# Sample attention: probabilities instead of values as the streamed operand, and the turning step dropped

## The reference

```python
def sparse_attend(q, k_sel, v_sel, dist, rel_bias):
    ...
    p = jax.nn.softmax(s, axis=-1)
    o = jnp.einsum('bthgn,btnhd->bthgd', p.astype(v_sel.dtype), v_sel)
    return o.reshape(B, T, A_WIDTH)
...
def mem_kv(mem, g_mem, w_xk, w_xv):
    m = rms_norm(mem, g_mem)
    mk = jnp.einsum('bmd,de->bme', m, w_xk).reshape(B, M, X_HEADS, X_HEAD_DIM)
    mv = jnp.einsum('bmd,de->bme', m, w_xv).reshape(B, M, X_HEADS, X_HEAD_DIM)
```

## Time and profile before

| | before |
|---|---|
| median of 3 runs | 2934.78 us |
| time of the profiled execution | 2934.78 us |
| its span | 2933.2 us |
| TensorE busy | 2777.6 us (95%) |
| VectorE busy | 1666.7 us (57%) |
| ScalarE busy | 1068.3 us (36%) |
| GpSimd busy | 212.6 us (7%) |
| mean granted TensorE clock | 0.974 |

### The profile page before, as it was taken

How to read it: one execution, slowest core, us unless ns; L and a number is a source line. 1 busy time by engine, 2 the same in 40 slices (tenths; PEclk the granted TensorE clock), 3 DMA queues, 4 the chain that set the end, 5 groups by cost and what they waited for, 6 DMA issues and landing times.

```text
span 2933.2 us, 46674 instructions
## 1 busy us (share of the span) xinstructions
PE 2777.6 (95%) x18724; PEld 2626.1 (90%) x18724; DVE 1666.7 (57%) x2355; ACT 1068.3 (36%) x1331; POOL 212.6 (7%) x303
## 2 busy tenths in 40 slices
PE   8989999899999999999989977989999999899995
PEld 7879887799999999998979856979999999899994
DVE  4464564477878777787454423365555555543334
ACT  4233454344444443444342323333232232333332
POOL 0102211011111111110000000000000000000002
PEclk9999999999999999999999988989999999999998
DMA  9756646745555454554545565535555555445553
GB/s 284 146 145 178 203 160 206 230 135 154 144 138 151 130 158 130 159 145 124 144 143 144 205 236 176 150 121 151 150 146 154 143 153 147 125 118 147 149 153 100
DMA packets 692709, 460.24 MB, mean 157 GB/s; under 512 B 13455, under 2 KB 661231, under 8 KB 686319
## 3 DMA queue, kind: packets, MB, share of 16 engines
q1 hardware_dynamic: 679952, 414.25, 49.4%
q0 software_dynamic: 8960, 30.47, 3.9%
q10 hardware_dynamic: 3712, 14.35, 1.3%
HBM read 429.91 MB, written 29.13 MB: 156 GB/s over the span
## 4 chain that ended last, share of the span: by engine, by line
PE 91%; DVE 3%; DMA 3%; ACT 2%; issue 1%; POOL 1%; POOLq 0%; ACTq 0%; SPq 0%; DVEq 0%
PE psum L580 19%; PE psum L586 19%; PE psum L577 19%; PE psum L816 4%; PE psum L1170 4%; PE psum L1171 3%; PE psum L1172 3%; PE psum L981 2%; PE psum L821 2%; PE psum L959 1%; PE psum L1072 1%; DMA ring<-in_w_in 1%; PE psum L962 1%; PE psum L955 1%; DMA h<-in_cache_mem_v 1%
## 5 line engine op out<-in xcount | busy, mean ns | idle before, releaser
L1211 DVE TENSOR_TENSOR w_low<-ring,w_high 128x2048 fp32r<-128x2048 f32 x292 | 675.5, 2314 | 387.3 <-ACT w_high L1841 386.9
L1841 ACT ACTIVATE w_high<-ring 128x2048 fp32r<-128x2048 f32 x294 | 561.6, 1911 | 776.1 <-PE psum L586 589.3
L577 PE MATMUL psum<-x_high,w_high 128*128 128x320 f32 x3808 | 609.5, 312 | 2.9 <-ACT w_high L1841 2.9
L580 PE MATMUL psum<-x_high,w_low 128*128 128x320 f32 x3808 | 601.5, 310 | 8.5 <-DVE w_low L1211 8.5
L580 PEld LDWEIGHTS psum<-x_high,w_low 128*128 128x128 f32 x3808 | 571.8, 189 | 9.1 <-DVE w_low L1211 9.0
L577 PEld LDWEIGHTS psum<-x_high,w_high 128*128 128x128 f32 x3808 | 568.9, 188 | 10.6 <-issue 3.5
L586 PE MATMUL psum<-h_low,w_high 128*128 128x320 f32 x3360 | 527.7, 309 | 0.0
L586 PEld LDWEIGHTS psum<-h_low,w_high 128*128 128x128 f32 x3360 | 502.4, 188 | 0.0
L1170 PE MATMUL psum<-y_high,w_down_high 128*128 128x320 f32 x704 | 219.7, 312 | 15.9 <-DVE w_low L1773 15.9
L1171 PE MATMUL psum<-y_low,w_down_high 128*128 128x320 f32 x704 | 217.9, 310 | 0.0
L1172 PE MATMUL psum<-y_high,w_low 128*128 128x320 f32 x704 | 217.9, 310 | 0.0
(11 more groups left out here) (394 smaller groups left out, 3033.6 us busy)
## 6 DMA issues: line engine op xcount, KB each, us to landing
ring<-in_w_in SPq DMA_DIRECT2D x128, 1024.0 KB, 5.6
ring<-in_w_up SPq DMA_DIRECT2D x88, 1024.0 KB, 5.6
ring<-in_w_down SPq DMA_DIRECT2D x64, 704.0 KB, 4.7
ring<-in_w_xk SPq DMA_DIRECT2D x16, 1024.0 KB, 5.3
ring<-in_w_xv SPq DMA_DIRECT2D x16, 1024.0 KB, 5.1
ring<-in_w_out SPq DMA_DIRECT2D x16, 1024.0 KB, 5.9
ring<-in_w_xq SPq DMA_DIRECT2D x16, 1024.0 KB, 5.8
ring<-in_w_xo SPq DMA_DIRECT2D x16, 1024.0 KB, 5.9
```

Of the source, the lines that this page charges most:

```text
L577: mm(out, w_hi[:, j % 2, k, :], x_hi[:, k, :], start=k == 0, stop=False)
L580: mm(out, w_lo[:, j, k, :], x_hi[:, k, :], start=False, stop=False)
L1211: V.tensor_tensor(w_lo[:, j], ring[:, j], w_hi[:, j % 2].bitcast(FP32), ALU.subtract).then_inc(N.slab_lo, 1)
L1841: F(w_hi[:, j % 2], ring[:, j], ACT.Copy).then_inc(N.slab_hi, 1)
```

## The change

The operands of `sample_weigh` are exchanged: the page of values (128 by 128) becomes the stationary operand, and the strip of 32 columns of `probT` is streamed. The result has columns of tokens at once, on all 128 partitions, each KV head in 32 columns of the bank. The number of matmul calls stays 12 for a sequence. The loop over heads is now the outer one. `sample_turn` and `sample_rows` go, with the semaphore `o_rows` and the buffer; `sample_weighed(b-1)` reads bank 6 and stands where `sample_rows(b-1)` stood. In the setup, the third step of `small_in` gets a semaphore of its own, `diag_ready`, and the later counts of `small_in` fall by one.

```diff
             def sample_weigh(b):
                 pe.wait_ge(N.p_evac, H + b + 1)
-                pe.wait_ge(N.o_evac, H)
-                pe.wait_ge(N.o_rows, b)
+                pe.wait_ge(N.o_evac, H + b)
                 pe.wait_ge(v_loaded[b % 2], 32 * (b // 2 + 1))
-                for pg in range(NPG):
-                    for h in range(KVH):
-                        mm(bank(6)[32 * h:32 * h + 32, 0:P], probT[:, b % 2, pg * P + 32 * h:pg * P + 32 * h + 32],
-                           v_page[:, b % 2, pg, h * P:(h + 1) * P], start=pg == 0, stop=False, skip_group_check=True)
                 for h in range(KVH):
-                    last = mm(bank(6)[32 * h:32 * h + 32, 0:P], probT[0:NS, b % 2, 2 * P + 32 * h:2 * P + 32 * h + 32],
-                              vN[0:NS, 2, h * P:(h + 1) * P], start=False, stop=True, skip_group_check=True)
+                    oc = slice(32 * h, 32 * h + 32)
+                    for pg in range(NPG):
+                        mm(bank(6)[:, oc], v_page[:, b % 2, pg, h * P:(h + 1) * P],
+                           probT[:, b % 2, pg * P + 32 * h:pg * P + 32 * h + 32], start=pg == 0, stop=False)
+                    last = mm(bank(6)[:, oc], vN[0:NS, 2, h * P:(h + 1) * P],
+                              probT[0:NS, b % 2, 2 * P + 32 * h:2 * P + 32 * h + 32], start=False, stop=True)
                 last.then_inc(N.pv_mm, 1)
-
-            def sample_turn(b):
-                pe.wait_ge(N.o_rows, b + 1)
-                pe.wait_ge(N.o_evac, H + b)
-                tr(bank(7)[:, 0:P], o_rows, ident).then_inc(N.pv_mm, 1)
...
-                if b > 1:
-                    sample_turn(b - 2)
                 memory_slab(R + H + b)
...
-            sample_turn(DB - 2)
             memory_slab(28)
             sample_weigh(DB - 1)
-            memory_slab(29)
-            sample_turn(DB - 1)
-            for n in range(30, 32):
+            for n in range(29, 32):
                 memory_slab(n)
...
             def sample_prob_out(b):
                 act.wait_ge(N.p_T, H + b + 1)
-                if b >= 2:
-                    act.wait_ge(N.pv_mm, ROWS_AT[b - 2])
-                else:
-                    act.wait_ge(N.pv_mm, H + b - 1)
+                act.wait_ge(N.pv_mm, H + b - 1)
...
-            def sample_rows(b):
-                act.wait_ge(N.pv_mm, ROWS_AT[b])
-                if b:
-                    act.wait_ge(N.pv_mm, TURN_AT[b - 1])
-                F(o_rows, bank(6)[:, 0:P], ACT.Copy).then_inc(N.o_rows, 1)
-
             def sample_weighed(b):
-                act.wait_ge(N.pv_mm, TURN_AT[b])
-                F(zq[:, :, SEQ + b * DT:SEQ + (b + 1) * DT], bank(7)[:, 0:P].rearrange("p (h t) -> p h t", t=DT), ACT.Copy)\
+                act.wait_ge(N.pv_mm, H + b + 1)
+                F(zq[:, :, SEQ + b * DT:SEQ + (b + 1) * DT], bank(6)[:, 0:P].rearrange("p (h t) -> p h t", t=DT), ACT.Copy)\
                     .then_inc(N.o_evac, 1)
...
-                pool.wait_ge(N.pv_mm, ROWS_AT[b - 2])
+                pool.wait_ge(N.pv_mm, H + b - 1)
                 v_loads(b)
...
-            pe.wait_ge(N.small_in, 3)
+            pe.wait_ge(N.diag_ready, 1)
...
-            last.then_inc(N.small_in, 1)
+            last.then_inc(N.diag_ready, 1)
```

More of the change, by code:

```diff
@@ L288, in hybrid_layer @@
         assert top[0] <= SQ_AT
-        o_rows = sqbuf[:, 1, 0:P]
         top[0] = CONST["causal"][0]
@@ L389, in hybrid_layer @@
             par_loaded pages_loaded wik_loaded ikpage_loaded rel_loaded slab_used bank_free act_step dve_step small_in
[L390 to L393, removed]
+            small_out sumsq_done diag_ready setup_mm setup_evac x_T x_evac rows_act h_ready m_T m_evac ik_mm ik_evac
+            idx_zero iw_evac idx_mm idx_free page_T page_evac dup_ready iqs_ready sidx_mm sidx_relu sidx_sum selected
+            out_T out_evac out_sent memo_sent bias_stored bias_loaded bm_ready s_mm s_read s_max s_exp s_prob p_T
+            p_evac pv_mm o_evac k_loaded0 k_loaded1 v_loaded0 v_loaded1 kt_T kt_evac b_staged f_gate gate_log gate_sum
             gate_ready f_ready logf_ready d_ready e_ready qk_ready a_mm aT_ready ke_T keN_ready s1_mm s1_ready st_mm
@@ L458, in hybrid_layer @@
         row_of_token = ident.rearrange("p (i h t) -> p h i t", h=4, t=DT)[:, 0:2]
-        ROWS_AT, TURN_AT = [H + 2 * b + 1 for b in range(DB)], [H + 2 * b + 2 for b in range(DB)]
         def two_back(it, per, g):
@@ L1285, in _ @@
             dve.wait_ge(N.small_out, 3)
-            dve.wait_ge(N.small_in, 5)
+            dve.wait_ge(N.small_in, 4)
             refine(small[:, 27:29], small[:, 11:13], small[:, 35:37]).then_inc(N.small_in, 1)
@@ L1875, in _ @@
             tile(2, iqT[:, 2])
-            act.wait_ge(N.small_in, 4)
+            act.wait_ge(N.small_in, 3)
             F(sqbuf[:, 0, 16:48], sqbuf[:, 0, 16:48], ACT.Exp).then_inc(N.small_out, 1)
@@ L1886, in _ @@
             F(w_ik_hi, w_ik, ACT.Copy).then_inc(N.side_high, 1)
-            act.wait_ge(N.small_in, 5)
+            act.wait_ge(N.small_in, 4)
             st.then(F(small[:, 19:21], small[:, 11:13], ACT.Ln))
@@ L1890, in _ @@
             tile(6, iqT[:, 6])
-            act.wait_ge(N.small_in, 6)
+            act.wait_ge(N.small_in, 5)
             for m in range(2):
@@ L2038, in _ @@
                     sample_prob_out(b - 1)
-                if b > 1:
-                    sample_weighed(b - 2)
                 memory_evac(n)
@@ L2046, in _ @@
                 else:
-                    sample_rows(b - 1)
+                    sample_weighed(b - 1)
                 send(n)
             sample_prob_out(DB - 1)
-            sample_weighed(DB - 2)
             def input_back(q):
@@ L2056, in _ @@
             high(30)
-            sample_rows(DB - 1)
+            sample_weighed(DB - 1)
             memory_evac(29)
@@ L2060, in _ @@
             high(31)
-            sample_weighed(DB - 1)
             memory_evac(30)
```

## The result

The changed kernel takes 2965.37 us (median of 4 runs, 2961.04 to 2966.59) against 2932.82 us: the ratio is 1.0109, with an interval of 1.0094 to 1.0125. It is slower by 1.1%, some 32 us, where 6.2 us were forecast. The direction was right and the size was wrong by a factor of five; the time lies above the range, which reached to 2946 us.

A forecast was written before the change was run, and what follows sets the result against it. The prediction took TensorE, busy 95% of the span and 91% of the chain, to bound the kernel. Longer weighing 5.52 + 0 + 1.55, less 0.88 us for turning, gave +6.2 us on 2934.78: 2941.0 us, range 2934 to 2946.

The forecast's parts named there:

- the room: TensorE's slack during the softmax, ahead of `sample_T`: weighing may grow 0.82 us a sequence for free, all beyond costs time.
- the slab behind the last weighing: After sequence 7's weighing: the slab takes 3.71 in place of 3.90 us, as a 0.19 us strips-to-full-array switch goes.
- The turning step: One transpose (line 902) between `sample_T` and the slab, removed: 0.11 us each, eight times, -0.88 us.
- ScalarE's copy: Copy of 0.26 us removed eight times, the other waits for weighing; ScalarE's 4.96 us idle covers both: cost 0.
- the queues: `v_loads` and `k_loads` during weighing: released as before, and a longer period gives the key pages more time; no cost.
- the reload: Load of `xT` after the last weighing, issued about 536.5 in place of 542.78 us, meets slab loads earlier: no cost.
- the semaphore: `diag_ready` in the setup takes the count of the same instruction: no cost.
- The new `sample_weigh`: Weighing's 24 instructions at 0.111 us: 2.66 against 0.92 us, 1.74 us more a sequence; 5.52 + 0 + 1.55 us in all.
- The clock: TensorE's granted clock in the stretch about 454 to 551 us: taken as full (1.00, 2.4 GHz), with no term for a fall.
- Streaming as the price: Rival for weighing: weight loads hide, 32 streamed columns cost no more than strips; -1.1 us, 2933.7 us, chance 0.07.
- the price of line 985: Rival for weighing: an intermediate 0.076 us an instruction; +0.3 us, 2935.1 us, chance 0.10.
- load and stream in turn: Rival for weighing: weight load and stream one after the other, 0.134 us an instruction; +10.6 us, 2945.4 us, chance 0.10.

The follow-up runs named there:

- strips four times: The kernel before with its whole old weighing (32 stationary, 128 streamed columns) done four times in each sequence: 2951.85 us, ratio 1.0058.
- Without new keys: The changed kernel with its four calls on new keys (64 rows) replaced by calls that read the first page again (128 rows): 2948.41 us, 1.0043.
- pages first: The changed kernel with the weighing's eight calls on pages (128 rows) ahead of the four on new keys (64 rows): 2950.93 us, 1.0057.

## Why the prediction was wrong

*What bounds the kernel, and the room.* Right. All the extra weighing beyond the 0.82 us came out on the chain; strips four times measured 15.3 us where this reckoning gave 15.8. One sign of it did not come: the slab behind the last weighing was to take 3.7 us, and took 3.90 (at 557.21) as before. So the 0.19 us were no switch from strips to the full array. Without new keys, where the last calls have 128 rows, that slab took 3.79 us: 0.11 of the 0.19 us is again a change from 64 to 128 rows. The chain gives the last weighing 3.39 us in place of 3.59, and the two deviations cancel; that this term comes out right is luck.

*The turning step.* Right: -1.1 us in the stretch, forecast -0.9.

*ScalarE's copy, the queues, the reload, the semaphore.* Right, all at nothing. ScalarE waited 1.8 us for the weighing, and its idle time before the slab's end swallowed that.

*The new `sample_weigh`.* The first term that failed. I priced 24 like instructions at 0.111 us. That price is right for like ones (0.116 without the new keys). But they aren't like: each head's pair of page calls is followed by one on 64 rows, and every change between 128 and 64 rows costs another 0.11 us. Seven of them lie inside the new weighing, where my sum had none. So it takes 3.6 us in place of 2.66; by the prediction's own sum the extra 2.67 us makes 6 x (2.67 - 0.82) + 0.9 + 2.5 - 0.9 = +13.6 us in place of +6.2. The diff shows the order of the loops, and the trace of before had a sign of the price in it. The chain in order of time, with calls on 128, 64 and 128 rows one after the other:

```profile
613.27 0.22 PE psum L1014 x2
613.49 0.36 PE psum L1015 x2
613.86 0.36 PE psum L1017 x2
```

The pair on 64 rows (line 1015) and the one behind it take 0.36 us in place of 0.22. I had used line 1017 for the distance of its two weight loads and not asked why the pair as a whole took longer. Part of those 0.14 us may be the waits that stand ahead of lines 1015 and 1017; the experiments show the price (0.11 us) without such waits.

*The clock.* The second step that failed, and the larger surprise: it was no term of the sum at all. The earlier trace rows were read as a property of the stretch (granted 1.00), when they are one of what TensorE does in it. Six falls at 1.6 us add 9.7 us. Together 13.6 + 9.7 = 23.3 us, against 23.5 measured in the stretch; the 9.7 are read from the same profile as the 23.5, so the sum checks the account and forecasts nothing.

That the falls come from the exchanged operands, with few columns streamed behind each load, is shown from two sides: the same kernel with 128 columns has none, and two kernels that weigh as long, with 128 columns in the old form, have none. The comparison rests on the counts of single profiles, none in each of four kernels with 128 columns against six or seven in the three profiles with 32 or 64 columns, head by head. What it is about the streamed columns was not taken apart further, and 64 of them did not help.

*The rest of the time.* Open. The first profile has 3.5 us more behind the stretch (2385.6 against 2382.1) and 0.6 us less ahead of it, and the medians (+32 us) are about 6 us above what this execution shows. One place where the executions differ is the part of the cross-attention. In the 40 us that begin 1210 us behind the end of the stretch the mean granted clock is 0.82 before, 0.65 in the change's first profile and 0.83 in its second. The clock falls there in every kernel, and it differs between two executions of the same one, so nothing here shows that the change or its delay moves it. I had expected the falls in the sequences to explain the spread of the times and they don't. What the executions near 2966 us look like no profile shows.

*The rivals.* Streaming as the price and the price of line 985 are refuted, load and stream in turn too, all by the 0.116 us for a plain instruction. Its 10.6 us were closer than my 6.2 by accident.

## What to carry to other kernels

When an operand exchange turns strips that share the array into full-width calls with a short stream, count the calls in their real order: neighbours to different strips overlapped here, a change in the number of rows cost about an instruction's time, and where both kinds occurred, it was cheaper to run each kind together. Do not take the granted clock of a stretch as given when the change alters what TensorE streams there: here it fell with TensorE busy at 100%, and the transposes and the slab behind paid 1.6 us each time. And look at the time in the shadow first: a step that seems dear (a copy, a transpose and a copy) was worth 1 us of 2935, and could be had by moving one call.

## What the runs showed of the hardware that was not expected

- A change between 128 and 64 rows of the stationary operand cost 0.11 us, with 32 columns streamed at full width (2.79 us for 24 instructions without a change, 3.59 with seven). A head's six instructions in one strip took the same 0.56 + 0.33 us. The weight loads, which otherwise start 0.11 us apart, did not overlap across it.
- Strips of 32 columns passed at 0.036 us when neighbours alternated; calls to one and the same strip showed the times of the full width.
- The granted clock fell from 1.00 to 0.50 behind 3.6 us of full-width weighing with 32 streamed columns, TensorE without idle time before and after; with 128 streamed columns it stayed at 1.00. A fall cost 1.6 us.
- A full-width instruction hardly cost less for streaming less: with pages first the 16 on pages took 1.90 us with 32 columns and 1.98 us with 128.
